# Hybrid decoder step on one core: w_in loaded by rows into four banks, attention 0 beside tile 1's projections, bulk loads in pieces, the samples' bias tables turned on chip

## The reference, cut to what matters

```
xn = rmsnorm(x);  q, k, v, u = xn @ w_in                 # 1024 -> 4 x 512; 1024 prompt rows, 32 sample rows
bias = rel_bias[bucket(q_pos - k_pos)];  lam = exp(lq1.lk1) - exp(lq2.lk2) + 0.2
attn = rmsnorm((softmax(q1 k1 + bias) - lam * softmax(q2 k2 + bias)) v)         # 4 heads, causal
pool = (moving mean of u over 2, 4, 8, 16 rows - u) @ pool_w
x = x + [attn | pool] @ w_out
xn2 = rmsnorm(x)                                          # experts: 8 heads, 16 of 128 x 128 each
idx, gate = top16 over keys of (xn2 @ wq) @ sub_keys;  x = x + sum(gate * gelu(xn2 . U[idx]) * V[idx])
x = x + sigmoid(rmsnorm(x) @ w_gate) * (p @ w_pl);  y = rmsnorm(x)
```

## Time and profile before

| | us |
|---|---|
| median of 3 runs | 3251.15 (3251.09 to 3255.97) |
| the profiled execution, by its own time | 3252.52 |
| its span, first to last instruction | 3250.5 |
| first gather issued by GpSimd | 218.52 |
| busy: PE, DVE, POOL, ACT | 2378.8, 2234.0, 1326.7, 952.1 |
| bytes moved | 1269.07 MB, of them 1133.76 MB by the software queue of the gathers |

### The profile page before, as it was taken

One profiled execution on the slowest core, in us unless ns is written; L12 is line 12 of the kernel. 1 busy time (PEld: TensorE's weight loads), 2 busy tenths in 40 slices (PEclk: granted clock), 3 DMA queues, 4 the chain that ended last, 5 costly groups with the idle time before them and its releaser, 6 DMA issues.

```text
span 3250.5 us, 53254 instructions
## 1 busy us (share of the span) xinstructions
PE 2378.8 (73%) x20824; PEld 952.7 (29%) x20824; DVE 2234.0 (69%) x5457; ACT 952.1 (29%) x2428; POOL 1326.7 (41%) x1143
## 2 busy tenths in 40 slices
PE   7779989648877878746876766666777676767666
PEld 3643333213333333312442212122222222222112
DVE  0356676667788788846667666577787777777764
ACT  1212233234344354312322222123332332233222
POOL 0014434333444434425564544344444454444441
PEclk9889999878889989868888887888888798789778
DMA  7559999989999999999999999999999999999994
GB/s 259 173 208 420 421 417 410 415 341 412 410 418 405 406 418 413 416 356 418 416 416 416 416 417 406 406 416 413 407 419 411 420 413 420 412 420 410 420 416 184
DMA packets 211731, 1269.07 MB, mean 390 GB/s; under 512 B 26480, under 2 KB 29832, under 8 KB 70544
## 3 DMA queue, kind: packets, MB, share of 16 engines
q0 software_dynamic: 159808, 1133.76, 85.0%
q1 hardware_dynamic: 50236, 131.61, 10.5%
q10 hardware_dynamic: 1436, 0.29, 0.0%
HBM read 1237.11 MB, written 28.65 MB: 389 GB/s over the span
## 4 chain that ended last, share of the span: by engine, by line
DMA 31%; PE 14%; DVE 7%; issue 2%; POOL 2%; DVEq 2%; ACT 1%; SPq 0%; POOLq 0%; ACTq 0%
DMA ring<-in_uv,idx 29%; PE sc L920 7%; DVE ring L1729 4%; PE sc L953 3%; POOL ring L1910 2%; PE route L895 1%; DVEq L1739 1%; DMA x_scratch<-x 1%; PE sc L922 1%; ACT diag L1287 1%; DMA front<-in_c_band_sp 1%; PE work L941 1%; PE sc L824 0%; ACT hgelu L1282 0%; DVE x L1781 0%
## 5 line engine op out<-in xcount | busy, mean ns | idle before, releaser
L1910 POOL DMA_INDIRECT ring<-in_uv,idx x1056 | 1249.2, 1183 | 1698.2 <-PE sc L922 1428.2
L920 PE MATMUL sc<-ring,diag 32*32 32x512 f32 x8192 | 1239.6, 725 | 695.6 <-ACT diag L1287 646.8
L1729 DVE CUSTOM_DVE_ANT_0 ring<-ring,xn_cur 128x1024 f32<-128x1024 f32 x1056 | 1279.5, 1221 | 633.7 <-DMA ring<-in_uv,idx 628.5
L922 PE MATMUL sc<-ring,diag 32*32 32x512 f32 x8192 | 1239.4, 725 | 0.0
L920 PEld LDWEIGHTS sc<-ring,diag 32*32 32x32 f32 x8192 | 273.1, 118 | 1472.7 <-ACT diag L1287 1024.1
L1282 ACT ACTIVATE hgelu<-hdot 128x2 f32<-128x2 f32 x528 | 107.5, 204 | 1817.1 <-DVE hdot L1729 1810.7
L1287 ACT ACTIVATE diag<-gate_d,hgelu 128x32 f32<-128x32 f32 x1056 | 281.7, 314 | 21.2
L922 PEld LDWEIGHTS sc<-ring,diag 32*32 32x32 f32 x8192 | 272.4, 118 | 1.5 <-issue 1.5
L498 PE MATMUL sc<-big,front 128*128 128x512 f32 x512 | 236.1, 608 | 4.3 <-DVE front L1383 3.6
L1282 ACT ACT_TABLE_LOAD x128 | 164.2, 1283 | 2.2
L895 PE MATMUL route<-big,xnT 128*128 128x256 f32 x560 | 136.7, 399 | 0.0
(11 more groups left out here) (264 smaller groups left out, 2303.6 us busy)
## 6 DMA issues: line engine op xcount, KB each, us to landing
front<-wqk_scratch SPq DMA_DIRECT2D x29, 1024.0 KB
ring<-in_uv,idx POOLq DMA_INDIRECT x1056
big<-in_w_in SPq DMA_DIRECT2D x4, 2048.0 KB, 17.9
wqk_scratch<-front SPq DMA_DIRECT2D x8, 1024.0 KB, 6.6
big<-wqk_scratch SPq DMA_DIRECT2D x8, 1024.0 KB, 18.9
x<-x_scratch SPq DMA_DIRECT2D x13, 512.0 KB
front<-in_x SPq DMA_DIRECT2D x8, 512.0 KB, 8.3
xnT<-in_wq_t POOLq DMA_DIRECT2D x8, 512.0 KB, 3.9
```

The source lines that it names most:

```text
L920: pe.matmul(sc[own, 0, :], diag[own, r, :], uv_rows[own, r, D:D + W4], start=opens_sum, stop=closes).then_inc(row_added[r], 1)
L922: pe.matmul(sc[other, 1, :], diag[own, r, :], uv_rows[own, r, D + W4:2 * D], start=opens_sum, stop=closes).then_inc(row_added[r], 1)
L1729: dve.tensor_tensor_reduce(uv_rows[:, k % RING, 0:D], uv_rows[:, k % RING, 0:D], xn_cur[:, :], 1.0, 0.0, ALU.mult, ALU.add, hdot[:, n % 2, ...
L1910: pool.indirect_dma_start(uv_rows[:, k % RING, :], None, uv, bass.IndirectOffsetOnAxis(ap=idx[:, n % PH, j:j + 1], axis=0)).then_inc(row_i ...
```

## The change

- w_in is loaded as 8 pieces of 128 full rows (1 MB each) in place of 4 blocks of columns. `project_first` runs over the pieces and adds each to all four outputs of tile 0, in four banks (A0, A1, S0, S1). Four constants of the twelve have a semaphore of their own (`first_in`), and tile 0 is turned ahead of the strips, which get four buffers.
- Attention 0 moves to front steps 1 to 12, beside tile 1's projections (one output a step, steps 1 to 4). Values come one step after the weights are turned. Folds go to steps 5 to 10 in pairs and 11 to 14 singly, in the order of heads 2 to 7, 0, 1; heads 0 and 1 are routed from where the fold left them, so their loads are gone. `route` and `choose` stand ahead of `front_step` in their steps, out of tile 1 at steps 15 and 16. `B[1].xr` leaves the ring.
- Bulk loads are issued in pieces in steps of their own: values 4, w_out 8 (twice), the samples' w_out 4, the gate's weights 12 in place of 5.
- The samples' bias tables are made by 4 small copies, 8 small TensorE operations and 2 copies from a bank, out of `biasw` in SBUF; the 36 small loads are gone. `load_samples` is at step 196, the samples' heads at 202, band and pool at 203 and 204.

```diff
-    return 10 * (t - EARLY) + 2 + 2 * o + half if t >= EARLY else -LEAD + 2 * t + o // 2
+    return 10 * (t - EARLY) + 2 + 2 * o + half if t >= EARLY else -LEAD + t * (1 + o)
...
-def fold_slot(hp):
-    return -LEAD + 4 + hp // 2
-
-ROUTE_0 = -4
+FOLD_HEADS = (2, 3, 4, 5, 6, 7, 0, 1)
+FOLDS = 2 * PH
+def fold_slot(j):
+    return -LEAD + (5 + j // 2 if j < 12 else j - 1)
+ROUTE_0 = -3
...
-        b = -LEAD + 2 + 3 * t
-        first = b + 2 + t
+        b = -LEAD + (1, 4)[t]
+        first = -LEAD + (2, 6)[t]
         scores = [[first + h] for h in range(H)]
         weights = [first + 2 + h for h in range(H)]
-        end = weights[-1]
-        return Attention(None, None, b, b + 1, b + 2, [(0, (t + 1) * T)], scores, weights, weights,
-                         (end + 1, end + 1), end + 2, (end + 3, end + 3 + (t == 0)))
+        values = [first + 3 + h for h in range(H)]
+        end = values[-1]
+        return Attention(None, None, b, b + 1, b + 2, [(0, (t + 1) * T)], scores, weights, weights, values,
+                         (end + 1, end + 1), end + 2, (end + 3, end + 4))
...
-        strip_sbuf = [cut(fr, 8192 + i * W4, W4) for i in range(2)]
-        onehot = cut(fr, 9728, W4)
+        lam_in = cut(fr, 7680, 4, QK)
+        strip_sbuf = [cut(fr, 8192 + i * W4, W4) for i in range(H)]
+        onehot = cut(fr, 7168, W4)
...
-                xr = [[xn_next[:, 0:W4], xn_next[:, W4:D]], [cut(a, 14848, W4), cut(a, 15360, W4)]][t]
-                avs = [xn_next[:, W4:D], cut(a, 15360, W4)][t]
+                xr = [[xn_next[:, 0:W4], xn_next[:, W4:D]], [cut(fr, 9216, W4), cut(fr, 8192, W4)]][t]
+                avs = [xn_next[:, W4:D], cut(fr, 8192, W4)][t]
...
-            return ((A0, A1) if t < EARLY else (S0, S1))[o % 2]
+            return (A0, A1, S0, S1)[o] if t == 0 else ((A0, A1) if t < EARLY else (S0, S1))[o % 2]
...
+            def project_first():
+                for o in range(4):
+                    b = project_bank(0, o)
+                    pe.wait_ge(free[b], opens(b, ("project", 0, o)))
+                for c in (TA, TB):
+                    pe.wait_ge(free[c], emptied(c, ("x", 0)))
+                for k in range(KD):
+                    pe.wait_ge(w_in_in[k], 16)
+                    for o in range(4):
+                        b, at = project_bank(0, o), COLUMNS[o] * W4
+                        mm = pe.matmul(bank[b], xTp[0][:, k, :], w_in_sb[:, k, at:at + W4],
+                                       start=(k == 0), stop=(k == KD - 1))
+                        if k == KD - 1:
+                            mm.then_inc(ready[b], 1)
...
+                if s == -LEAD:
+                    project_first()
...
+            def sample_bias():
+                pe.wait_ge(bias_rep, 1)
+                pe.wait_ge(free[S0], opens(S0, "sample bias"))
+                for h in range(H):
+                    pe.transpose(bank[S0][:, h * DS:(h + 1) * DS], biasw[0:DS, h, 0:T], ident[0:DS, 0:DS])
+                for h in range(H):
+                    mm = pe.matmul(bank[S0][0:NS, (H + h) * DS:(H + h + 1) * DS],
+                                   b_rep[0:DS, h, :], ident[0:DS, 0:DS], start=True, stop=True)
+                mm.then_inc(ready[S0], 1)
...
-                if s == C0 + 2:
+                if s == C0 + 1:
+                    sample_bias()
+                if s == C0 + 8:
                     turn_sample_heads()
-                if s == C0 + 3:
+                if s == C0 + 9:
                     sample_band()
-                if s == C0 + 4:
+                if s == C0 + 10:
...
+                if n < 2:
+                    for b in (A0, A1):
+                        pe.wait_ge(free[b], emptied(b, ("fold", FOLDS - 1)))
+                elif n < STREAMED:
+                    pe.wait_ge(wst_in[n % 2], 16 * (n // 2))
...
+            pe.wait_ge(first_in, 16 * 4)
+            pe.wait_ge(x_in[0], 16)
+            turn_x(0, xt[0])
...
+                (ident[:, :], c_ident), (relb[0:BUCKETS, :], rel_bias),
+                (onehot[0:BUCKETS + 1, :], c_onehot[:, STRIP0:STRIP0 + STRIPW]), (g_attn, norm_attn_g),
+            ):
+                act.dma_start(dst, src).then_inc(first_in, 16)
...
-                if t == 0 and o < 2:
-                    act.wait_ge(strip_out[o], 16 * 2)
+                if t == 0:
+                    act.wait_ge(strip_out[o], 16)
                 if t == EARLY and o == 0:
                     act.wait_ge(ready[S1], filled(S1, ("out", EARLY - 1, 1)))
+                    act.wait_ge(x1_out, 16 * 2 * EARLY)
...
-                if s == C0 + 1:
+                if s == C0:
                     dve.wait_ge(ready[S1], filled(S1, ("out", NT - 1, 1)))
+                    for h in range(H):
+                        ins = dve.tensor_copy(b_rep[0:DS, h, :].rearrange("p (b i) -> p b i", b=DB),
+                                              biasw[0:DS, h, T:T + DS].unsqueeze(1).to_broadcast([DS, DB, DS]))
+                    ins.then_inc(bias_rep, 1)
+                if s == C0 + 2:
                     dve.memset(q_bd, 0.0).then_inc(q_zero, 1)
                     dve.tensor_copy(bf_T.rearrange("p (h i) -> p h i", h=H), far.unsqueeze(2).to_broadcast([T, H, DS]))
-                if s == C0 + 5:
+                    dve.wait_ge(ready[S0], filled(S0, "sample bias"))
+                    dve.tensor_copy(b_raw, bank[S0][:, 0:H * DS])
+                    dve.tensor_copy(bx_raw[0:NS, :], bank[S0][0:NS, H * DS:2 * H * DS]).then_inc(free[S0], 1)
+                if s == C0 + 11:
...
+                if s in (ROUTE_0, ROUTE_0 + 2):
+                    choose((s - ROUTE_0) // 2)
                 front_step(s)
-                for hp in range(2 * PH):
-                    if s == fold_slot(hp):
-                        keep_fold(hp)
-                if s == ROUTE_0 - 1:
+                if s == -LEAD:
+                    constants()
+                for j in range(FOLDS):
+                    if s == fold_slot(j):
+                        keep_fold(j)
+                if s == ROUTE_0 - 3:
...
-            pool.wait_ge(w_in_in[1], 16)
+            pool.wait_ge(w_in_in[KD - 1], 16)
             for i in range(2):
                 pool.dma_start(keys_sb[i], keys_t[i * PH:(i + 1) * PH].rearrange("h d k -> d h k")).then_inc(keys_in, 16)
-            for hp in range(2 * PH):
-                if hp >= 2:
-                    pool.wait_ge(ready[A1], filled(A1, ("fold", hp - 2)))
-                pool.dma_start(wq_st[hp % 2], wq_t[hp * T:(hp + 1) * T, :]).then_inc(wq_in[hp % 2], 16)
+            for j in range(FOLDS):
+                if j >= 2:
+                    pool.wait_ge(ready[A1], filled(A1, ("fold", j - 2)))
+                hp = 2 * FOLD_HEADS[j // 2] + j % 2
+                pool.dma_start(wq_st[j % 2], wq_t[hp * T:(hp + 1) * T, :]).then_inc(wq_in[j % 2], 16)
...
-                if k == RING - 1:
-                    pool.wait_ge(x1_out, 16 * 2 * EARLY)
...
-            def load_w_in(o):
-                c = COLUMNS[o]
-                sp.dma_start(w_in_sb[:, :, c * W4:(c + 1) * W4],
-                             w_in[:, c * W4:(c + 1) * W4].rearrange("(k p) n -> p k n", p=T)).then_inc(w_in_in[o], 16)
-            def load_halves(dst, src, s):
-                for c in range(2):
-                    cols = slice(c * W4, (c + 1) * W4)
-                    sp.dma_start(dst[:, :, cols], src[:, cols].rearrange("(k p) n -> p k n", p=T)).then_inc(s, 16)
+            def load_w_in(k):
+                sp.dma_start(w_in_sb[:, k, :], w_in[k * T:(k + 1) * T, :]).then_inc(w_in_in[k], 16)
+            def load_rows(dst, src, k, s):
+                sp.dma_start(dst[:, k, :], src[k * T:(k + 1) * T, :]).then_inc(s, 16)
...
-            def load_back():
-                sp.dma_start(cut(big_a, 4096, NT, W4), nv_p.rearrange("(k p) n -> p k n", p=T)).then_inc(vals_in, 16)
-                load_halves(B[EARLY].wo, w_out, w_out_in)
+            def load_old_values(i):
+                tiles = slice(2 * i * T, 2 * (i + 1) * T)
+                sp.dma_start(cut(big_a, 4096 + 2 * i * W4, 2, W4), nv_p[tiles, :].rearrange("(k p) n -> p k n", p=T)
+                             ).then_inc(vals_in, 16)
...
-                if n < 2:
+                if n < 4:
                     for i in range(2):
                         sp.wait_ge(stage_out[i], 16 * PH // 2)
-                else:
-                    sp.wait_ge(ready[RT], filled(RT, n - 2))
+                sp.wait_ge(ready[RT], filled(RT, n - 2))
...
+                sp.wait_ge(ready[S0], filled(S0, "sample bias"))
...
-                with nc.allow_non_contiguous_dma(reason="small bias tables"):
-                    for h in range(H):
-                        base = h * T * STRIPW
-                        sp.dma_start(b_raw[:, h * DS:(h + 1) * DS],
-                                     strip_view(base + near0, [[1, T], [STRIPW - 1, DS]]),
-                                     allow_slow_non_contiguous=True).then_inc(bT_in, 16)
```

(55 more changed lines are left out.)

213 lines of the change are left out of this document (98 added, 115 removed).

## The result

| | before | after |
|---|---|---|
| median of 4 runs, us | 3251.12 (3251.01 to 3255.97) | 3208.45 (3205.74 to 3212.70) |
| profiled execution, its own time / span | 3252.52 / 3250.5 | 3209.12 / 3207.1 |
| first gather issued | 218.52 | 190.98 |

The ratio is 0.9866, with a 95% interval of 0.9849 to 0.9883: 43 us faster, where 42 was forecast. The page of the changed kernel, against the earlier trace rows: the third slice rises from 208 to 289 GB/s, and the slices at 341 and 356 are gone.

A forecast was written before the change was run, and what follows sets the result against it. After the front the kernel was taken to be bound by DMA bytes. Front 20.5, wst load -2.5 and dips 24 sum to 42 us off the profiled 3252.5, set against a median 1.4 lower: 3209 us, range 3194 to 3233.

The forecast's parts named there:

- Constants: Front's start: four gating constants land at 8.5 us, bounds 4.5 and 15.0; projection starts at 17.6.
- The turn: Front, from tile 0 to tile 1: about 3.9 us against 2.3 before; project(1) starts at 52.0.
- Steps 1 to 4: Front: four outputs make 27.8 us, attention work beside them adds 5.0; step 5 starts at 84.8.
- Steps 5 to 10: Front's fold steps: 57.7 us, bounds 36 and 63; out of tile 0 starts at 142.5.
- Steps 11 to 15 and route: Front's end: 20.3, 10, 7.0 and 2.3 us, then route and choose 15.2 and 0.7; first gather at 198.
- wst(2): Start of the stream: 1 MB load joins the full part, -2.5 us; route(2) done 18 us after first gather, no stall.
- First dip: 650 to 725 us: w_out in pieces after step 63's stores gives back 13.5 of 15.0 us.
- Second dip: 1420 to 1440 us: samples' loads asked for six steps later, giving back 10.5 of 11.6 us.
- The fixed cost: Rival, 28 more bulk loads: each pays 2.4 us, 67 us against a gain of 42, 3276 us; chance 0.08.
- The rival of the front that stays long: Front: fold steps keep 10.5 us, constants land at 13, first gather at 212; gain 28, 3223 us; chance 0.15.
- The jam of steps 66 to 75: Rival, dips shrink little: SyncE runs ahead, issuing w_out, values and wst together; gain 24, 3227 us; chance 0.12.
- The signs named beforehand: Profile after: first L498 under 20, first gather near 198, no window under 400 GB/s from 600 to 750 us.

The follow-up runs named there:

- the values experiment: Changed kernel with the values of tiles 0 and 1 computed again in the step in which their weights are turned: 3229.24 us, ratio 0.9931.
- The sooner load: Changed kernel with wst for n = 2 loaded one step sooner, ahead of tile 1's x stores: 3204.13 us, ratio 0.9858.
- the first experiment: Changed kernel with values and w_out all issued at step 62 again, still in pieces: 3218.38 us, ratio 0.9903.
- the kernel that has the stall again: Changed kernel with values and w_out pieces all issued at step 62, ahead of the samples' stores: 3218.38 us, ratio 0.9903.
- the changed kernel's columns: Changed kernel with w_in loaded again in four 2 MB column blocks, tile 0 projected output by output: 3207.28 us, ratio 0.9863.

## Why the prediction was right, and where it wasn't

- **What bounds it.** Right: a bytes-bound stream with three places to gain. Each rise of the staircase is one of them.
- **Constants** (8.5, bounds 4.5 and 15). Measured 10.6, and 5.4 if w_in isn't beside them. Projection started at 20.66, forecast 17.6: 2.1 us are the constants, and 1.0 is the time between the strips and projection, which the earlier trace rows show (25.95 is 10.0 behind 15.92) and the sum left out. "TensorE, not the load, sets the pace" held.
- **The turn** (3.9). 5.6: the two table reloads, 1.28 us each, weren't counted. Taking one away, with the exponential and what VectorE does behind it, gave 1.9 back.
- **Steps 1 to 4** (32.8). 34.3. Step 5 came at 90.30, 5.5 later than the 84.8 forecast.
- **Steps 5 to 10, the mis-sized term of the sum** (57.7). 50.7, from 90.30 to 140.97. "I stay near the upper one, as the chain from scores ... to the fold's copies is untouched" was too cautious in its size, though the chain it names is there. The wait of 18.7 us went, as the values experiment shows, but 9.5 us of waiting for the fold's copies came in its place: in all TensorE stood 25.8 us from 88 to 171.88 before and stands 14.2 from 90.30 to 140.97 now, 11.6 less and not 18.7. What more than made up for this is the speed of TensorE's operations, which the forecast held fixed. Ten of the twelve folds left in these steps take 1.95 to 2.06 us; before, the sixteen took 2.7 in the mean and up to 3.62, at a granted clock of 0.89, 0.77 and 0.66 in the three windows, where the changed kernel has 1.00, 0.89 and 0.89. Twelve folds at the old mean would have taken 6 us more.

  The slow folds are those behind a stand: the fold of 3.62 us at 153.21 came behind one of 4.7 us and ran at a granted clock of 0.50, the one of 1.95 at 107.60 at 1.00, and in the changed kernel itself the two folds behind stands of 2.7 and 2.9 us took 3.14 and 3.40. With the values' wait put back, half of the 18 us that the stretch grew by is longer operations. The 4 us that the forecast added for the first heads and tile 0's norm aren't seen either; TensorE's operations besides the folds took 10.1 us where 14.5 were before.
- **Steps 11 to 15 and route** (39.5, 15.9). 36.0 and 14.0, 5.4 less together; 1.3 of it is route(0), 3.69 us instead of 5.01, and the rest is a little in each part. Front: 5.5 - 7.0 - 5.4 = -6.9, so 191 in place of 198.
- **wst(2)** (-2.5, no stall). The stream lost 2.3 by gather 40, so the size was right. TensorE did stand 12.4 us for the load; route(2) was done 19 us after the first gather, not 18, and the first rows came 19.9 after it against 17.4 before. The gathers in flight covered that, as forecast: 428 GB/s from 195 to 200 us and 424 from 200 to 205. The sooner load gave 4.3.
- **First dip** (13.5). 14.3, or 13.0 by the means, no window of 25 us under 414 from 600 to 725, and the reason given (order of issue) is the one that the first experiment shows.
- **Given back** (nothing forecast). 4.4 us between steps 84 and 196, or 2.3 by the means. I took filled dips to be pure gain. The windows at 730 and 950 us show 323 and 271 GB/s with TensorE busy 10.00 us of 10, and the kernel that has the stall again makes up there: 14.0 behind becomes 8.9 at step 196. But the size is near what traces differ by: over the same columns the other kernels of the experiments, whose dip is filled, move by up to 2.7 us against the changed one. And the kernel before has such a window too, 327 GB/s from 1120 to 1130 us.
- **Second dip** (10.5). 9.4, or 7.8 by the means. Here the prediction named one stall; in fact there were two, one hiding the other, and the change needed both edits.
- **The fixed cost** (rival, 0.08). Falls: 81 more transfers cost 9.4 us, not 194. The rival of the front that stays long falls too. The jam of steps 66 to 75 isn't seen either: SyncE does run ahead there and issues four pieces of w_out together, but in 2.87 us.
- **The signs named beforehand.** Most came: scores of tile 0 between the projections, no wait of the values, out of tile 0 at 140.97, no wait of `pooled(2)`, no issue of 46 us. Two didn't. Projection starts at 20.66, not under 20. And from 725 to 750 us the stream is at 376 GB/s, where no window under 400 was to be; in a window of ten us, at 730, it is even under the 350 that would have made the prediction wrong. The dip that it meant, from 650 to 700, is gone all the same.

Open: whether and why the stretch after the first dip gives back 2 to 4 us. That TensorE, with more expert rows behind it, meets its attention work there as a bottleneck fits the windows, but no run took that work away, so it is argued and not shown. Open too is what attention 0 beside tile 1's projections gives by itself.

## What to carry to other kernels

What a bulk load cost others here hung on the step in which it was issued, and hardly on how it was cut: find what stands behind a bulk load or behind many small ones, and which engine waits for that. Count a stall on TensorE with the work beside it, which ran slower for it here; and before two stalls near each other are costed, undo them both, since one can hide the other. Where an engine's stream is bound by bytes, look at the windows behind a filled dip as well, since part of it may be given back there.

## What the runs showed of the hardware

- Eight single-element loads took SyncE 17.5 to 28.1 us beside full gathers, and 2.8 us once the gathers had run dry.
- Four small constants on ScalarE's queue landed at 5.4 us with only x's load beside them, 10.6 beside w_in by rows (8.7 beside w_in by columns); all twelve took 28.5 us by rows, 15.0 by columns in the kernel before, and no more than 20.05 with the changed kernel's columns.
- Splitting 27 loads into four cost 9.4 us, 0.12 us a transfer in the mean; in the trace the cost shows at two waits of TensorE, and not where no engine waited.
- TensorE's folds of 16 records took 1.95 us at a granted clock of 1.00 and 3.62 at 0.50, the slow ones behind stands of 2.2 to 4.7 us.
- A reload of ScalarE's function table took 1.28 us, and the next activation started 0.02 us behind it. Taking a reload and an exponential of 0.20 out from between two operations that TensorE waits for gave 1.5 us of its path back, and 0.4 more on VectorE. The Trainium skill, page ScalarE: Activation LUTs, section "What ACT_TABLE_LOAD costs", gives the same 1.28 us for the load and 1.38 more for a drain, 2.66 in all; the load agrees, and the drain isn't seen in these traces.
